# Moving two gate evaluations and two weight splits of the last attention one unit earlier on ScalarE

## The reference

```python
h = rms_norm(x, norm_g)
u_a, g_a, q_b, k_b, v_b, f_b, g_b, q_m, g_m = split_cols(h @ w_in)
y_a = pool_mixer(u_a, w_pool, pool_scale)          # 256 channels
y_b = fox_attention(q, k, v, logf)                 # 8 heads of 64, causal, with forget gates
y_m = memory_attention(q_mh, k_m, v_m)             # 4 heads of 64 over 256 memory tokens
mixed = concat([y_a * silu(g_a), y_b * silu(g_b), y_m * silu(g_m)])
x = x + mixed @ w_out
```

## Time and profile before

| | |
|---|---|
| median of 3 runs | 1556.49 us (1556.03 to 1559.03) |
| profiled execution, its own time | 1556.49 us |
| span of its trace | 1554.7 us |
| PE busy | 1495.1 us (96%) |
| DVE busy | 897.6 us (58%) |
| ACT busy | 611.3 us (39%) |
| POOL busy | 511.0 us (33%) |
| mean granted clock of PE | 0.995 |

### The profile page before, as it was taken

One profiled execution on the slowest core, in us unless ns is written; L12 is line 12 of the kernel. 1 busy time (PEld: TensorE's weight loads), 2 busy tenths in 40 slices (PEclk: granted clock), 3 DMA queues, 4 the chain that ended last, 5 costly groups with the idle time before them and its releaser, 6 DMA issues.

```text
span 1554.7 us, 21457 instructions
## 1 busy us (share of the span) xinstructions
PE 1495.1 (96%) x8174; PEld 1252.0 (81%) x8174; DVE 897.6 (58%) x1315; ACT 611.3 (39%) x768; POOL 511.0 (33%) x380
## 2 busy tenths in 40 slices
PE   7999999999999999999997999999999999999999
PEld 5888888798888888889775898888888897777767
DVE  7778686566665552136686476666540265465741
ACT  3555455234222322236555253222321255455540
POOL 3000001214545545441311315545454524432222
PEclk9999999999999999999998999999999999999999
DMA  7511121322222232331201203232322312312111
GB/s 224 135 55 55 55 82 55 136 82 82 85 104 89 100 108 81 135 109 65 90 37 55 82 28 108 81 108 81 108 99 90 122 55 81 136 62 92 68 55 55
DMA packets 22583, 137.22 MB, mean 88 GB/s; under 512 B 2488, under 2 KB 4840, under 8 KB 7280
## 3 DMA queue, kind: packets, MB, share of 16 engines
q1 hardware_dynamic: 17280, 124.79, 22.5%
q10 hardware_dynamic: 5232, 11.45, 2.9%
HBM read 132.02 MB, written 4.21 MB: 88 GB/s over the span
## 4 chain that ended last, share of the span: by engine, by line
issue 58%; POOL 25%; PE 14%; ACT 1%; DVE 1%; DMA 0%; DVEq 0%; POOLq 0%; ACTq 0%; SPq 0%
POOL WL L444 16%; POOL WL L453 9%; PE pair L480 4%; PE pair L482 3%; PE pair L481 3%; PE pair L1048 1%; PE pair L1035 1%; PE pair L967 1%; PE pair L1025 1%; ACT WH L1155 0%; DMA RAW<-stream 0%; DVE PL L2150 0%; PE pair L1018 0%; ACTq L1486 0%; ACT PL L1490 0%
## 5 line engine op out<-in xcount | busy, mean ns | idle before, releaser
L444 POOL TENSOR_TENSOR WL<-RAW,WH 128x512 fp32r<-128x512 f32 x240 | 327.6, 1398 | 490.3 <-ACT WH L1155 490.3
L480 PE MATMUL pair<-AH,WH 128*128 128x512 f32 (+1 forms) x1240 | 472.5, 381 | 14.4 <-POOL WL L444 11.4
L481 PE MATMUL pair<-AL,WH 128*128 128x512 f32 (+1 forms) x1240 | 463.0, 373 | 0.0
L482 PE MATMUL pair<-AH,WL 128*128 128x512 f32 (+1 forms) x1240 | 462.9, 373 | 0.0
L1155 ACT ACTIVATE WH<-RAW 128x2048 fp32r<-128x2048 f32 x108 | 206.6, 1914 | 475.1 <-PE pair L482 461.0
L453 POOL TENSOR_TENSOR WL<-RAW,WH 128x512 fp32r<-128x512 f32 x136 | 183.2, 1379 | 534.5 <-ACT WH L1155 534.5
L480 PEld LDWEIGHTS pair<-AH,WH 128*128 128x128 f32 x1240 | 233.6, 188 | 59.7 <-POOL WL L444 11.4
L482 PEld LDWEIGHTS pair<-AH,WL 128*128 128x128 f32 x1240 | 233.5, 188 | 41.8
L481 PEld LDWEIGHTS pair<-AL,WH 128*128 128x128 f32 x1240 | 233.8, 189 | 40.8 <-issue 1.9
L1944 DVE TENSOR_SCALAR CA<-pair,PAR 128x512 f32<-128x512 f32 x88 | 67.3, 806 | 148.1 <-PE pair L482 145.1
L480 PE MATMUL pair<-GH,WH 128*128 (+2 forms) x416 | 150.4, 361 | 0.0
(11 more groups left out here) (245 smaller groups left out, 2005.6 us busy)
## 6 DMA issues: line engine op xcount, KB each, us to landing
RAW<-stream SPq DMA_DIRECT2D x115, 1024.0 KB, 4.8
H<-x_t SPq DMA_DIRECT2D x3, 1024.0 KB, 8.9
bias_rows<-ROWS ACTq DMA_DIRECT2D x1, 2048.0 KB, 24.8
BIAS<-bias_rows ACTq DMA_DIRECT2D x1, 2048.0 KB, 7.7
FBC<-forget_rows ACTq DMA_DIRECT2D x4, 512.0 KB, 3.9
out<-H ACTq DMA_DIRECT2D x8, 256.0 KB, 2.0
H<-x_t SPq DMA_DIRECT2D x2, 512.0 KB, 6.4
CON<-consts ACTq DMA_DIRECT2D x1, 513.5 KB, 4.8
```

The source lines that it names most:

```text
L444: pool.tensor_tensor(WL[w][:, part], RAW[raw][:, part], WH[w][:, part].bitcast(F32), ALU.subtract).then_inc(w_lo, 1)
L480: pe.matmul(out_, wh, xh, start=start, stop=False, skip_group_check=shared)
L481: pe.matmul(out_, wh, xl, start=False, stop=False, skip_group_check=shared)
L482: return pe.matmul(out_, wl, xh, start=False, stop=stop, skip_group_check=shared)
```

## The change

```diff
@@ gate(j, second), ACT
                 act.activation(SG[:, (2, 3, 0, 1)[j]], bk(6), ACT.Silu)
                 act.activation(second, bk(7), ACT.Copy if j < 2 else ACT.Silu).then_inc(sg_made, 1)
                 act.preload_act_table_set("natural_log_exp_and_others")
+                split_next(E_CHUNK[j])
@@ the loop over u, ACT
                 if u in (5, 9):
                     gate((u - 5) // 4, PU[:, (u - 5) // 4])
-                    split_next(E_CHUNK[(u - 5) // 4])
-                if u == 14:
+                if u == 13:
                     gate(2, SG[:, 4])
-                if u == 15:
-                    split_next(E_CHUNK[2])
-                if u == 17:
+                if u == 16:
                     gate(3, SG[:, 5])
-                if u == 18:
-                    split_next(E_CHUNK[3])
```

## The result

The changed kernel takes 1567.84 us (median of 4, 1566.43 to 1569.63) against 1556.55 us (median of 4, 1556.03 to 1559.03): ratio 1.0080, 95% interval 1.0065 to 1.0094. In a second round on another occasion it took 1568.18 us against 1556.46, ratio 1.0075 (1.0059 to 1.0091), where 1568 to 1569.5 was expected. It is 11 to 12 us slower by these medians; all twenty-two executions of it on record together have a median of 1569.2 us, 12.6 above. The forecast was 1570.6 with a range from 1563.5 to 1573.5.

A forecast was written before the change was run, and what follows sets the result against it. The prediction took the chain expo, weights, turn, and how far expo is ahead of PE, as what matters. Terms of 4.98 + 3.53 + 5.6 = 14.1 us on 1556.5 gave 1570.6 us, range 1563.5 to 1573.5.

The forecast's parts named there:

- Gate 2's term: Gate 2 and its split ahead of expo(15) on ACT: turn(15) on PE starts 4.98 us later.
- bound without POOL: Lower bound of a gate's delay if POOL doesn't slow DVE's weights pair: 3.42 us at turn(15), 1.74 more at turn(18).
- Gate 3's term: Gate 3 and its split ahead of expo(18) on ACT: turn(18) on PE starts 3.53 us later still.
- A slowdown in proportion: At unit 18's weights on DVE: the alternative that POOL stretches the 384-wide pair to 2.1 us, 0.4 less than taken.
- The clock's term: PE behind turn(15) and turn(18): longer idle times lower the clock to 1.2 GHz, losing 2.8 us each, 5.6 together.
- The sum: Whole kernel: 4.98 + 3.53 + 5.6 = 14.1 us slower, 1570.6 us.
- What costs nothing: Same instructions, earlier splits and chunk loads, no PE wait at turn(19); from there PE is back to back as before.
- The table load: Each gate's chain on ACT: by the page's drain 1.4 us longer, sum 2.7 higher; the forecast went by the row, without drain.
- No drop of the clock: Rival 1, PE at both turns: stalls come, clock stays high or drops once briefly; + 8.5, 1565.0 us; chance 0.17.
- No meeting of DVE and POOL: Rival 2, DVE's weights pairs: multiplications don't meet POOL and the clock stays; + 5.2, 1561.7 us; chance 0.09.
- Idle time of turn(18) belongs to gate 3: Rival 3: the 3.06 us ahead of turn(18) are gate 3's time on ACT and go; 1553.4 us; chance 0.04.
- Hidden: Rival 4: ACT's work is hidden, since expo is 7.9 us ahead of its use at unit 18; 1556.5 us; chance 0.04.

The follow-up runs named there:

- run with the unsaid splits: Changed kernel, each moved split done on ACT without telling POOL, and again at its old place telling POOL: 1565.42 us against 1556.61 for the kernel before, ratio 1.0058.
- kernel that was kept busy: Changed kernel plus overwritten extra PE matmuls, 22 ahead of score(17) and 24 ahead of turn(18): 1565.55 us, against 1568.18 for the changed kernel.
- gate 2 with filler: Kernel before with gate 2 and its split in iteration 13, first half of gate 3's chunk on PE from 15 to end of 14: 1557.75 against 1556.46 us.
- gate 3 only: Kernel before with gate 3 and its split moved to iteration 16, gate 2 and its split unmoved: 1562.24 against 1556.61 us, ratio 1.0042.
- gate 2 only: Kernel before with gate 2 and its split moved to iteration 13, gate 3 and its split unmoved: 1564.3 against 1556.61 us, ratio 1.0056.
- gates without splits: Kernel before with both gates one iteration earlier, splits left in iterations 15 and 18: 1560.38 against 1556.61 us, ratio 1.0019.
- splits alone: Kernel before with gates left at 14 and 17, each split moved right behind its gate: 1558.82 against 1556.58 us, ratio 1.0011.

## Why the prediction was right, point by point

**Gate 2's term.** Predicted 4.98 us, measured 4.93 (table). The pattern of gate 1 carried over to a hundredth except for the weights pair, 2.37 us for 2.44. That its bound without POOL would be 3.42 was confirmed by the run with the unsaid splits.

**Gate 3's term.** Predicted 3.53 us, measured 3.45, by way of a 2.46 us pair for the 384-wide unit. A slowdown in proportion, 2.1 us, is ruled out. Its bound without POOL, 1.74 us, measured 1.72: in the run with the unsaid splits turn(18) waits 4.78 us where it waited 3.06.

**The clock's term** is the one that was mis-sized: predicted 2.8 us at each place, measured 2.52 and 2.06 in the table, 4.6 together in place of 5.6 (4.4 by the kernel that was kept busy). I had taken over that 6.2 of 6.7 us at 1.2 GHz lie behind PE's restart, as around 827 us. Here the clock falls earlier in the longer idle time, 1.4 and 2.2 us ahead of the restart, and those microseconds cost nothing. What is left of 6.8 us is 5.4 and 4.6, and at 1.8 times the duration that loses 2.4 and 2.1 us. Nor did a longer idle time cost more clock in these runs: 3.06 us were followed by a loss of 2.6 (gate 2 with filler), 6.51 by one of 2.3 (gate 3 only) or 2.1.

**The sum.** 14.1 us predicted, 13.0 in the two traces of the changed kernel, 11.3 to 11.7 in the medians. The first difference is the clock's term. The second is not clear of noise: the interval of the ratio is 10.1 to 14.6 us, and the twenty-two executions together give 12.6. A part of it may have a cause that the runs point at: the 3.06 us ahead of turn(18) are a borderline case. Five profiles have this idle time (3.06 or 3.07). In that of the kernel before the clock stays high; in three others (gate 2 only, gates without splits, splits alone) it falls for 3.4 us, in the fourth (gate 2 with filler) for 6.8. If other executions of the kernel before have that low stretch, its profile was on the lucky side and its median holds both cases. As there is one trace of it, this is not shown.

**What costs nothing** held: turn(19) to the end takes 46.05 against 46.04 us, and no wait for a low part appeared in the changed kernel.

**The table load.** The rule of the Trainium skill's page "ScalarE: Activation LUTs", section "What ACT_TABLE_LOAD costs" (some 1.4 us of drain beside the load) is not borne out here: the load starts 0.02 us after the activation before it has ended (1473.16 and 1473.18 at gate 2), the split 1.29 after the load's start, and 4.38 and 4.39 us from SiLU to expo leave no room for a drain.

**The rivals.** No drop of the clock: fell, 0.50 twice. No meeting of DVE and POOL: fell. Idle time of turn(18) belongs to gate 3: fell in the gate-3-only run. Hidden: fell.

## What to carry to other kernels

An instruction that is moved up on an in-order engine brings its own wait along: here the gate waits for PE, and from then on everything queued behind it does too. Before moving one, look at what stands behind it, how much slack that has, and whether the waiting engine has filler between; filler and gate have to be moved together. Fillers at both places turned the change's +11 us into +1.8; the best version (-2.5) moves gate 2 with its filler, leaves gate 3 where it was, and moves PE's work there instead. A pattern that already stands elsewhere in the same trace gave the delay of its copy to a tenth of a microsecond here (4.98 and 3.53 predicted, 4.93 and 3.45 measured); what the clock adds to it was off by a microsecond.

## What the runs showed of the hardware

A weights pair that meets POOL's pieces with both of its multiplications takes 2.37 to 2.51 us whether it is 384 or 512 wide (0.75 and 0.88 alone), and a 256-wide one 2.1 (0.62 alone). In the changed kernel's trace each multiplication ends 0.2 or 0.3 us after a piece of POOL, so DVE waits for whole pieces, not for a share. The page "SBUF — State Buffer" of the Trainium skill, section "SBUF: two separate sides", calls the port pair of the two engines an exclusive lock and not a split of bandwidth; the trace agrees.

Which idle times lower PE's clock is not fixed by their length near 3 us: 3.06 us did in four profiles of five. Such places early in the program go with the differences between executions of one kernel: of 23 executions of the kernel before, the three with a mean clock of 0.997 have spans of 1551.8 to 1552.4 us, the four with 0.992 spans of 1558.6 to 1559.1. The start of turn(11), which no experiment changed, lies between 1445.99 and 1451.84 us in the profiles: at 1446.0 and 1446.4 in the two that have 10.2 us of low clock before it, between 1448.2 and 1448.8 in the four with 13.6 (that of before among them), between 1451.3 and 1451.9 in the seven with 20.4. That is about 0.5 us for each microsecond at 1.2 GHz, and larger than most effects measured here; a comparison inside the trace, from a common event on, is free of it.
